# A two-block network in fp32 on one core: the order of the recurrence, the step sizes, the norm's rescaling and the ends of the hybrid mixers

## What is computed

```python
def rg_lru(x, w_a, b_a, w_x, b_x, lam):            # first block, layer 0, inside mix0
    r = sigmoid(block_diag(x, w_a, b_a))
    i = sigmoid(block_diag(x, w_x, b_x))
    log_a = 8.0 * r * log_sigmoid(lam)
    a = exp(log_a)
    u = sqrt(-expm1(2.0 * log_a)) * (i * x)
    h_t = a_t * h_{t-1} + u_t                      # a scan over the 512 tokens
def mixer_gla_rglru(h, ...):                       # mix0
    q, k, v, g, lr, xr, xg = split(h @ w_in)
    o = rmsnorm(chunked_linear_attention(q, k, v, log_f(lr))) * silu(g)
    y = rg_lru(conv(xr), ...) * gelu(xg)
    return concatenate([o, y]) @ w_out
def hybrid_mixer(h, ...):                          # mix2, layers 0 and 1 of the second block
    q_a, kv_a, k_pe, z, xbc, dt_raw = split(h @ w_in)
    attn_out = causal_attention(...)
    dt = softplus(dt_raw + dt_bias); a = -exp(a_log)
    y = ssd_chunked(xs, dt, a, bm, cm) + d_skip * xs   # exp(+-cumsum(dt * a)) in chunks of 128
    yg = rmsnorm(y * silu(z), over each of 2 groups) * ssd_norm_w
    return concatenate([attn_out, yg]) @ w_out
def swiglu_2(h, w_gate_up, w_down): ...            # ffn2, on (rmsnorm(x) * (1 + sc2) + sh2)
```

## Time and profile before

| | us |
|---|---|
| median of 3 runs | 3278.98 |
| the 3 runs | 3278.98, 3273.4, 3279.07 |
| the profiled execution | 3279.2 |
| its span | 3277.5 |
| PE busy | 3237.9 (99%) |
| DVE busy | 1819.8 (56%) |
| ACT busy | 1156.2 (35%) |
| POOL busy | 83.0 (3%) |

### The profile page before, as it was taken

The page is one execution under the profiler, slowest core; times in us unless marked ns, Lnnn a source line. Parts: engine busy times, 40 slices in busy tenths (PEclk is TensorE's granted clock), DMA queues, the critical chain, the costliest instruction groups (busy, mean ns, idle before and its releaser), DMA issues.

```text
span 3277.5 us, 37001 instructions
## 1 busy us (share of the span) xinstructions
PE 3237.9 (99%) x15264; PEld 2692.5 (82%) x15264; DVE 1819.8 (56%) x2615; ACT 1156.2 (35%) x1615; POOL 83.0 (3%) x124
## 2 busy tenths in 40 slices
PE   8999999999999999999999999999999999999999
PEld 7888877888888888887888888888788888878887
DVE  6664366666446664366566635876433368663332
ACT  5222253322233222263322223654322245442221
POOL 1000000000000000000000000100000010000000
PEclk9999999999999999999999999999999999999999
DMA  5443322444334443322244433211232322023222
GB/s 158 154 141 119 109 77 77 129 149 143 109 106 126 132 154 111 98 87 78 77 146 146 131 105 105 81 52 39 90 103 87 100 83 82 9 90 103 90 97 71
DMA packets 334237, 339.84 MB, mean 104 GB/s; under 512 B 12406, under 2 KB 329112, under 8 KB 334072
## 3 DMA queue, kind: packets, MB, share of 16 engines
q1 hardware_dynamic: 332112, 333.80, 32.1%
q0 software_dynamic: 1728, 3.62, 0.4%
q10 hardware_dynamic: 232, 0.06, 0.0%
HBM read 335.36 MB, written 2.10 MB: 103 GB/s over the span
## 4 chain that ended last, share of the span: by engine, by line
PE 86%; DVE 9%; ACT 4%; issue 1%; DMA 0%; DVEq 0%; SPq 0%; ACTq 0%
PE ps L135 85%; DVE wl L100 2%; DVE ar L100 1%; DVE ar L108 1%; ACT ar L95 1%; ACT wh L95 1%; PE ps L138 1%; ACT L95 1%; DVE ar L117 1%; DVE hl L108 0%; DVE T L108 0%; DVE ada L108 0%; DVE T L100 0%; DMA raw<-in_ffn_w 0%; ACT hh L95 0%
## 5 line engine op out<-in xcount | busy, mean ns | idle before, releaser
L135 PE MATMUL ps<-hh,wl 128*128 128x512 f32 x2760 | 1088.5, 394 | 10.4 <-DVE hl L108 5.9
L100 DVE TENSOR_TENSOR wl<-raw,wh 128x1024 fp32r<-128x1024 f32 (+2 forms) x547 | 654.1, 1197 | 763.5 <-ACT wh L95 763.1
L135 PE MATMUL ps<-hh,wh 128*128 128x512 f32 x2760 | 1077.0, 390 | 0.0
L135 PE MATMUL ps<-hl,wh 128*128 128x512 f32 x2760 | 1076.8, 390 | 0.0
L95 ACT ACTIVATE wh<-raw 128x1024 fp32r<-128x1024 f32 (+2 forms) x547 | 560.5, 1027 | 463.2 <-PE ps L135 461.9
L135 PEld LDWEIGHTS ps<-hh,wl 128*128 128x128 f32 x2760 | 519.9, 188 | 122.0 <-issue 11.4
L135 PEld LDWEIGHTS ps<-hh,wh 128*128 128x128 f32 x2760 | 519.8, 188 | 109.3
L135 PEld LDWEIGHTS ps<-hl,wh 128*128 128x128 f32 x2760 | 520.2, 188 | 104.7 <-issue 0.6
L135 PE MATMUL ps<-uh,wl 128*128 128x512 f32 x1056 | 411.8, 390 | 0.0
L135 PE MATMUL ps<-uh,wh 128*128 128x512 f32 x1056 | 410.9, 389 | 0.0
L135 PE MATMUL ps<-ul,wh 128*128 128x512 f32 x1056 | 410.8, 389 | 0.0
(11 more groups left out here) (242 smaller groups left out, 2729.1 us busy)
## 6 DMA issues: line engine op xcount, KB each, us to landing
raw<-in_ffn_w SPq DMA_DIRECT2D x120, 1024.0 KB, 5.3
raw<-in_w_ada SPq DMA_DIRECT2D x48, 1024.0 KB, 5.2
raw<-in_w_gate_up SPq DMA_DIRECT2D x44, 1024.0 KB, 5.1
raw<-in_m_w_in SPq DMA_DIRECT2D x26, 1024.0 KB, 5.4
raw<-in_w_down SPq DMA_DIRECT2D x16, 1024.0 KB, 5.0
raw<-in_ffn_w SPq DMA_DIRECT2D x16, 768.0 KB, 4.2
raw<-in_w_in SPq DMA_DIRECT2D x12, 1024.0 KB, 5.4
raw<-in_m_w_out SPq DMA_DIRECT2D x8, 1024.0 KB, 4.9
```

Source lines behind the costliest of these rows:

```text
L100: return self.issue(lambda e: e.tensor_tensor(out, a, b, op))
L135: return self.issue(lambda e: e.matmul(out, l, r, start=start, stop=stop, skip_group_check=True))
```

## The change

There are seven edits.

1. mix0's recurrence goes in pairs of tiles. PE's gate tiles come as r0, r1; i0, i1; and the last four together, all one piece sooner at the end. ACT does Exp, Tanh and Square of tiles 0 and 1 at v0, the four other gates and Exp, Tanh, Square of tiles 2 and 3 at v1, and a Sqrt over two tiles at v2 and another at v3. DVE does `ix` and `om` of a pair at v1 and at v2, multiplies and scans tiles 0 and 1 at v3, ahead of `by_rows`, and tiles 2 and 3 at g0.
2. mix2's bank `ystat` becomes two banks. The first tile of it, POOL's power over it and al0 come before the last mean squares; al1 stands behind the transposes `cat`. The tiles c are taken in the order 0, 4, 1, 5, 2, 3, 6, 7.
3. ffn2's entry: DVE reads the spread norm from PSUM, ACT's copy R stands behind its eight tiles, and DVE's low part of (w1, 1) behind all eight tiles instead of in the middle.
4. ACT takes one Exp of a constant right behind the Silu of z (z3), so that a table load stands there.
5. dt and its product with a come before xb6, the scan and `ends` before z2, instead of behind z3.
6. In the chain `states` ACT's high part of `ad` stands behind the exponentials and turned(4), turned(5); DVE's low part of it and the spreading X3 stand behind decayed(3).
7. `rescaled` goes from ahead of the first small products (their parts cl, their copies) to a place between sums(1) and product xb2; a wait of DVE for itself is added in heads_turned(0).

```diff
     def lru():
-        for a in range(2):
-            for t in range(4):
+        for some in (((0, 0), (0, 1)), ((1, 0), (1, 1)), ((0, 2), (0, 3), (1, 2), (1, 3))):
+            for a, t in some:
                 b = banks.take((s, "gx", a, t))
                 pe.wait_ge(misc_in, (s, "in"))
                 pe.wait_ge(worked, (s, "conv", t))
                 pe.mm(b[:, :], wbd[:, a, t, :], A(34 + t)).then_inc(formed, (s, "gx", a, t))
-                if t % 2:
-                    yield 1
+            yield 1
...
         def frame_means(t):
             for k in range(4):
-                done = pe.mm(bs[:, 4 * t + k:4 * t + k + 1], E2[t % 2][:, 128 * k:128 * k + 128], ones[:, 0:1])
+                done = pe.mm(bs[:, 4 * (t % 2) + k:4 * (t % 2) + k + 1], E2[t % 2][:, 128 * k:128 * k + 128], ones[:, 0:1])
...
         weigh(3)
-        bs = banks.take((s, "ystat"), hold=True)
+        bs = banks.take((s, "ystat", 0))
         pe.wait_ge(worked, (s, "y01"))
         frame_means(1)
         yield 1
...
         yield 1
         frames(3)
         yield 1
+        bs = banks.take((s, "ystat", 1), hold=True)
         pe.wait_ge(squared, (s, "y", 2))
         frame_means(2)
         yield 1
+        pe.wait_ge(pooled, (s, "v8", 0))
+        along((s, "al", 0), sm[:, 0:4])
+        yield 1
         pe.wait_ge(squared, (s, "y", 3))
         frame_means(3)
-        banks.drop((s, "ystat"))
-        yield 1
-        yield 1
-        pe.wait_ge(pooled, (s, "v8"))
-        for g in range(2):
-            along((s, "al", g), sm[:, 4 * g:4 * g + 4])
+        banks.drop((s, "ystat", 1))
+        yield 1
...
-    begin(s, [("out", 0), ("out", 1)], ch, cl, (s, "c"), (0, 4, 1, 5, 2, 6, 3, 7))
+    pe.wait_ge(pooled, (s, "v8", 1))
+    along((s, "al", 1), sm[:, 4:8])
+    begin(s, [("out", 0), ("out", 1)], ch, cl, (s, "c"), (0, 4, 1, 5, 2, 3, 6, 7))
...
         return
     begin(s, names)
-    act.wait_ge(formed, ("al", s))
-    act.f(R[:, :], ps(("al", s))[:, :], ACT.Copy).then_inc(left(("al", s)), ("al", s))
     for t in range(8):
         if t == 5:
             step(G_of[(s, "w1", 1)])
         modulated(s, 3, t)
+    act.f(R[:, :], ps(("al", s))[:, :], ACT.Copy).then_inc(left(("al", s)), ("al", s))
...
-        for a in range(2):
-            for t in range(4):
+
+        def gates(*some):
+            for a, t in some:
                 act.wait_ge(formed, (s, "gx", a, t))
                 act.wait_ge(formed, (s, "gate", 1))
                 act.f(A((30 + t, gi[t])[a]), ps((s, "gx", a, t))[:, :], ACT.Sigmoid,
                       bias=col(("lru_ba", "lru_bx")[a], t)).then_inc(left((s, "gx", a, t)), (s, "gx", a, t))
-                if t % 2:
-                    yield 1
-        while dec in act.side:
-            yield 1
-        for t in range(4):
-            act.wait_ge(*left_of((s, "gx", 0, t)))
-            act.wait_ge(worked, "clam")
-            act.own()
-            act.f(A(ga[t]), A(30 + t), ACT.Exp, scale=clam[:, t:t + 1]).then_inc(curved, (s, "a", t))
-        for t in range(4):
-            act.wait_ge(curved, (s, "a", t))
-            act.f(A(30 + t), A(30 + t), ACT.Tanh, scale=clam[:, t:t + 1]).then_inc(curved, (s, "th", t))
-        yield 1
-        for t in range(4):
-            act.wait_ge(curved, (s, "a", t))
-            act.f(bufs[t][:, :], A(ga[t]), ACT.Square).then_inc(curved, (s, "a2", t))
-        yield 1
-        yield 1
-        act.wait_ge(worked, (s, "om", 3))
-        act.f(A(30, 4), A(30, 4), ACT.Sqrt, scale=-1.0).then_inc(curved, (s, "sq"))
+
+        def decays(t0):
+            for t in (t0, t0 + 1):
+                act.wait_ge(*left_of((s, "gx", 0, t)))
+                act.wait_ge(worked, "clam")
+                act.wait_ge(worked, (s, "rest", 1))
+                act.f(A(ga[t]), A(30 + t), ACT.Exp, scale=clam[:, t:t + 1]).then_inc(curved, (s, "a", t))
+            for t in (t0, t0 + 1):
+                act.wait_ge(curved, (s, "a", t))
+                act.f(A(30 + t), A(30 + t), ACT.Tanh, scale=clam[:, t:t + 1]).then_inc(curved, (s, "th", t))
+                act.f(bufs[t][:, :], A(ga[t]), ACT.Square).then_inc(curved, (s, "a2", t))
+
+        def roots(t0):
+            act.wait_ge(worked, (s, "om", t0 + 1))
+            act.f(A(30 + t0, 2), A(30 + t0, 2), ACT.Sqrt, scale=-1.0).then_inc(curved, (s, "sq", t0))
+
+        gates((0, 0), (0, 1))
+        yield 1
+        gates((1, 0), (1, 1))
+        yield 1
+        decays(0)
+        yield 1
+        gates((0, 2), (0, 3), (1, 2), (1, 3))
+        decays(2)
+        yield 1
+        roots(0)
+        yield 1
+        roots(2)
         yield 1
...
+        act.wait_ge(worked, (s, "de"))
+        act.f(cd, al, ACT.Exp, scale=-1.0).then_inc(curved, (s, "cd"))
+        act.f(de, de, ACT.Exp).then_inc(curved, (s, "de"))
+        yield 1
+        turned(4)
+        turned(5)
         act.wait_ge(worked, (s, "ad"))
         act.wait_ge(used, G_of[(s, "z", 3)])
         act.f(hl[:, 6, :], A(43), ACT.Copy).then_inc(hi_part, (s, "ad"))
-        act.wait_ge(worked, (s, "de"))
-        act.f(cd, al, ACT.Exp, scale=-1.0).then_inc(curved, (s, "cd"))
-        act.f(de, de, ACT.Exp).then_inc(curved, (s, "de"))
-        yield 1
-        turned(4)
-        turned(5)
...
             act.own()
             act.f(A(24, 4), A(24, 4), ACT.Silu).then_inc(curved, (s, "z"))
+            act.f(sm[:, 38:39], one, ACT.Exp)
...
     begin(s, names)
     dve.wait_ge(formed, (s, "c"))
     dve.copy(t8[4][:, 0:2], ps((s, "c"))[:, 0:2]).then_inc(left((s, "c")), (s, "c"))
-    dve.wait_ge(*left_of(("al", s)))
-    for t in modulated(s, 3, R[:, :]):
-        if t == 5:
-            step(G_of[(s, "w1", 1)])
+    dve.wait_ge(formed, ("al", s))
+    for t in modulated(s, 3, ps(("al", s))[:, :]):
+        pass
+    step(G_of[(s, "w1", 1)])
...
+
+        def inputs(t0):
+            for t in (t0, t0 + 1):
+                dve.wait_ge(*left_of((s, "gx", 1, t)))
+                dve.wait_ge(worked, (s, "conv", t))
+                dve.tt(A(gi[t]), A(gi[t]), A(34 + t), MUL).then_inc(worked, (s, "ix", t))
+            for t in (t0, t0 + 1):
+                dve.wait_ge(curved, (s, "a2", t))
+                dve.wait_ge(curved, (s, "th", t))
+                dve.stt(A(30 + t), bufs[t][:, :], 1.0, A(30 + t), ADD, MUL).then_inc(worked, (s, "om", t))
+
+        def scans(t0):
+            for t in (t0, t0 + 1):
+                dve.wait_ge(curved, (s, "sq", t0))
+                dve.wait_ge(worked, (s, "ix", t))
+                dve.tt(A(gi[t]), A(gi[t]), A(30 + t), MUL).then_inc(worked, (s, "u", t))
+                dve.own()
+                dve.scan(A(34 + t), A(ga[t]), A(gi[t])).then_inc(worked, (s, "h", t))
+
+        yield 1
+        yield 1
+        yield 1
+        inputs(0)
+        yield 1
+        inputs(2)
+        yield 1
+        scans(0)
+        yield 1
+        scans(2)
+        yield 1
...
     convolved(0)
-    if l == 0:
-        for t in range(4):
-            rescaled(t)
...
     product(s, "z", 1)
     sums(1)
+    if l == 0:
+        for t in range(4):
+            rescaled(t)
     product(s, "xb", 2)
...
     def heads_turned(hd):
         Q = A(3) if hd % 2 else R[:, :]
         dve.wait_ge(formed, (s, "qt", hd))
+        if hd == 0:
+            dve.own()
         dve.copy(Q[0:96, :], ps((s, "qt", hd))[0:96, :]).then_inc(left((s, "qt", hd)), (s, "qt", hd))
...
         dve.tt(de, TKt[:, 1], al, SUB).then_inc(worked, (s, "de"))
-        dve.wait_ge(hi_part, (s, "ad"))
-        dve.tt(hl[:, 7, :], ad, hl[:, 6, :].bitcast(F32), SUB).then_inc(lo_part, (s, "ad"))
-        dve.wait_ge(pooled, (s, "X3"))
-        shares(X3, 64).then_inc(worked, (s, "X3"))
...
         decayed(3)
+        dve.wait_ge(hi_part, (s, "ad"))
+        dve.tt(hl[:, 7, :], ad, hl[:, 6, :].bitcast(F32), SUB).then_inc(lo_part, (s, "ad"))
+        dve.wait_ge(pooled, (s, "X3"))
+        shares(X3, 64).then_inc(worked, (s, "X3"))
...
         yield 1
         weigh(3)
         yield 1
+        k = (s, "ystat", 0)
+        dve.wait_ge(formed, (s, "ys", 1))
+        dve.ts(sm[:, 0:4], ps(k)[:, 4:8], D / 256, MUL, s2=EPS, op1=ADD).then_inc(left(k), k)
         frames(2)
         yield 1
         frames(3)
         yield 1
         yield 1
+        scaled(0)
+        scaled(1)
+        yield 1
+        k = (s, "ystat", 1)
         dve.wait_ge(formed, (s, "ys", 3))
-        dve.ts(sm[:, 8:20], ps((s, "ystat"))[:, 4:16], D / 256, MUL, s2=EPS / 2,
-               op1=ADD).then_inc(left((s, "ystat")), (s, "ystat"))
+        dve.ts(sm[:, 8:16], ps(k)[:, 0:8], D / 256, MUL, s2=EPS / 2, op1=ADD).then_inc(left(k), k)
         dve.own()
-        dve.ts(sm[:, 0:4], sm[:, 8:12], EPS / 2, ADD).then_inc(worked, (s, "v8", 0))
-        dve.tt(sm[:, 4:8], sm[:, 12:16], sm[:, 16:20], ADD).then_inc(worked, (s, "v8"))
+        dve.tt(sm[:, 4:8], sm[:, 8:12], sm[:, 12:16], ADD).then_inc(worked, (s, "v8"))
         yield 1
     def scaled(t):
...
         if name is None:
             next(ssd, 0)
             return
```

(39 more changed lines are left out.)

38 lines of the change are left out of this document (11 added, 27 removed).

## The result

The changed kernel takes 3262.26 us (median of four runs, 3253.7 to 3263.01), 0.9946 times the kernel before (95% interval 0.9932 to 0.9960). So the direction and the bulk were right and the gain, 16.7 us by the medians and 17.7 by the ratio, was larger than the 12.3 expected. The profiled execution took 3262.16 us with a span of 3260.4, 17.1 less than before.

What follows compares the result with a forecast made beforehand. PE was taken as the bound, busy 3237.9 of 3277.5 us, with 39.6 us of waits plus the granted clock to win. 3279.2 - 2.6 - 3.4 - 4.2 - 0.9 - 1.6 + 0.4 = 3266.9 us, range 3261.5 to 3274.5.

Steps and rivals of the forecast that it cites:

- mix0's order, -2.6: mix0: output pair starts at 529.0 instead of 531.55, despite a new wait of some 2.1 us before the states.
- The clock behind it, -3.4: mix0's output pair: with the 3.49 us idle gone, the half clock behind it goes too, 3.4 us.
- the first rival: mix0: half clock follows the new 2.1 us wait or remaining idle; 3.4 us come back, 3270.3; chance 0.25.
- Behind z3, -4.2: mix2 behind z3: PE's waits of 1.00 and 0.79 us both end, 2.1 us in each layer.
- rescaled, -0.9: mix2's first small products, layer 0: four instructions leave the copies' way; wait falls from 1.12 towards layer 1's 0.26.
- ffn2's entry, -0.8 a layer: ffn2's entry: of PE's waits of 1.36 and 0.39 us, 0.8 come back in each layer.
- mix2's end, +0.4: mix2's end: al0 no longer hides DVE's last 0.43 us of values(7); +0.2 us a layer.
- half clocks I leave as they are: mix2's end: half-clock stretches, 6.8 us in layer 1 and 3.4 in layer 0, taken as unchanged.
- the rival that named al0 and al1: mix2's end: new order removes half clocks at 2244 and 2848, -1.7 or -3.4 or both; 3265.2 to 3261.8; chance 0.10.
- The shifts did add up: Rival said they don't: next late release takes mix0's gain and half of that behind z3; 3275.0; chance 0.10.
- The rival with a load at twice its row: mix0: each ACT table load costs 2.57 us, output pair begins at 532.8 with its half clock; 3274.2; chance 0.06.
- no step was lost there: mix0: rival said a late first Sqrt stalls PE, costing steps of 5.5 us, 3275.8 to 3286.8; chance 0.04.

Runs made afterwards that it cites:

- experiment 7: Changed kernel with ad's parts and X3 ahead of the turned tiles again and rescaled back where it was: 3258.02 us, ratio 0.9938.
- experiment 11: Changed kernel without the dummy Exp, mix2's end as before, three thrown away 384-column fp32 matmuls ahead of al0 per layer: 3264.92 us, ratio 0.9966.
- experiment 12: Kernel before with only the new end of mix2: 3269.98 us, ratio 0.9979.
- experiment 9: Changed kernel with by_rows ahead of the scans and 32 thrown away transposes ahead of the first product: 3254.41 us, ratio 0.9933.

## Why the forecast came out as it did

The terms of order came to -8.9 in the forecast and -10.2 in the traces, the terms of the clock to -3.4 and -6.6. The total hides errors of opposite sign: mix0 gave 2.4 less than forecast, the other places 6.9 more.

- **mix0's order, -2.6.** Right in mechanism and near in size: 2.2 between two executions without a stretch. The hand layout had scans(0) from 473.35 and by_rows to 479.8; they stand from 472.71 and to 479.12. The wait of 2.1 us it added is the 2.22 above.
- **The clock behind it, -3.4.** Half right: the stretch at 531 went, but one of 3.4 us came behind the new wait, as the first rival said; net 1.4. A stretch of 6.8 us is worth 2.6 to 3.2 us by place and one of 3.4 mostly 1.3 to 1.6, not quite their halves. In mix0 PE was not full in it (6.15 of 6.8 us); at mix2's end it was, so that is not the whole reason.
- **Behind z3, -4.2.** The term was too small by 1.2: 2.7 a layer. Edit 6 gives 0.85 of it (experiment 7). The brackets of the earlier trace rows, 1.00 and 0.79, understate what stands between starts, and the 0.38 us wait at decayed(3) was counted as staying and does stay. The dummy Exp, on which I let the gain rest in part, adds nothing to the earlier step sizes.
- **rescaled, -0.9.** 1.2 to 1.3: the difference of two brackets, 1.12 and 0.26, leaves out the small waits behind.
- **ffn2's entry, -0.8 a layer.** 0.7 each by order; the wait for the low part came, with 0.20 instead of 0.3 to 0.5.
- **mix2's end, +0.4 and "half clocks I leave as they are".** This is the step that failed. The order is worth nothing, and the clock, which the sum put at nothing, gives 1.0 to 1.6 us a layer between the two profiled executions. I looked for idle ahead of each stretch and, finding none there, took the stretch as given; the rival that named al0 and al1 had 0.10 and was right on this place. The unbroken run of matmuls of 1 and 64 columns brings the lower clock there: parted with nothing else changed it had a stretch in 0 of 4 cases, unparted in 10 of 10. The two profiled executions understate it. The eight old ends without experiment 11's have seven stretches of 6.8 us and one of 3.4, the 18 new ones three of 3.4; at the prices by place (3.0 and 1.5) that is an estimate of 2.6 us a layer, 5 a run, which fits experiment 12. For mix0's clock the same count gives about 1.4, as traced.
- **ffn2's stretches at 2299 and 2907** (2.6 us together by the clock) were not forecast and went in this execution. With the old end of mix2 three of five executions have both and two have neither; behind the new or parted end 3 of 22 places have one. Whether the new end takes them away or chance did is open.
- **The other rivals.** The shifts did add up: no place gave less by order than forecast but mix0, by 0.4, and ffn2's entry, by 0.1 a layer. ACT started the first Sqrt at 469.31 us and needed 1.06, so it ended 0.5 us ahead of the layout's 470.9, and no step was lost there.
- **The table loads.** The rival with a load at twice its row was wrong. In the changed kernel ACT goes from a load to the gates in 1.29 us, right behind another function's instruction:

```profile
457.34 1.05 ACT L95 ACTIVATE wh<-raw 128x1024 fp32r<-128x1024 f32 x1
458.41 1.28 ACT L95 ACT_TABLE_LOAD   x1
459.70 2.43 ACT L95 ACTIVATE ar<-ps,VT 128x512 f32<-128x512 f32 x4
```

The 1.38 us of drain of the Trainium skill ("ScalarE: Activation LUTs", "What ACT_TABLE_LOAD costs") shows behind none of the four loads of this stretch whose next function follows at once, 1.29 to 1.30 us from the load's start; the next function behind the fifth waits 11 us for DVE, and tells nothing.

What stays open: why a stretch comes in one execution and not in the next behind the same instructions at the same distances (mix1 5 of 16, near 2655 9 of 16), and whether filling the 2.2 us wait helps, for which one execution without a stretch stands against six of eight unfilled ones without. The traces give a hint that no run tested: just ahead of the stretches near 2655 and 2299, and of the one at 73 us in experiment 9, PE does 16 matmuls of one column in some 1.8 us (2653.66 to 2655.43 in the changed kernel), again few columns and no long idle.

## What to carry to other kernels

List where the granted clock was low before costing an edit, and read what PE did ahead of each: in this kernel long idle, or a run of matmuls with few columns. Either is a cost that an edit can move without moving an instruction of the critical path, and thrown away wide matmuls in such a place tell its price (0.9986 of the time for the long idle, no stretch in four cases for the narrow run). Profile two executions of a kernel before explaining a difference under its own scatter, and read pieces of 1 us from their place in the trace, not from the time.

## What the runs showed of the hardware

- PE busy without a gap can fall to the lower clock: at the old end of mix2, matmuls of 1 and 64 columns, in 10 of 10 cases; with four matmuls of 128 columns in their midst in 0 of 2, with eight in 0 of 2. Columns, plain fp32 and the weight load of each were not told apart.
- Idle of 3.5 us was followed by it in 3 of 4 executions and 2.2 us in 2 of 8, so idle doesn't settle it alone; with the idle filled or gone it followed in none of five. The scatter of one kernel's times (3253.7 to 3263.01) goes with it: its execution at a mean granted clock of 0.999 took 3253.7, those at 0.996 3262 to 3263.
- A table load on ACT took 1.28 us and the next function began 1.29 us after the load's start, also right behind another function, in the four loads around mix0's gates in the changed kernel whose next function had its data (1.30 in one of them).
